# Layer 0's modulation in linear stages, seven-product down projections in the first block, rotations ahead of the heads' sums, memory in four transfers

## The chip, the cores and the metric

One core of one Trainium2 chip runs the kernel: TensorE (PE) multiplies, VectorE (DVE), ScalarE (ACT) and GpSimd (POOL) do the elementwise work, SyncE (SP) issues the transfers from HBM. The metric is the device time of one execution in microseconds. The kernel before takes 2530.83 us, the median of 3 runs (2528.49 to 2532.82).

## The reference

Batch 1, T=256 tokens, D=1024, all in fp32. A first block of two layers works on `x` with a memory `mem` of 256 tokens: a mixer (layer 0 forgetting and differential attention, layer 1 an mLSTM), attention over the memory, and a convolutional FFN; then a final norm. A second block of two layers works on `x` and a context `ctx` (512 tokens together), with three branches (latent attention MLA, grouped attention GQA, a Fourier branch), gates, and again an FFN; each of its norms and residual additions is modulated by vectors computed from the conditions `c` and `c_ctx`.

```python
for layer in range(2):                    # first block
    x = x + mixer[layer](rms_norm(x, mix_norm[layer]))
    x = x + memory_cross_attention(rms_norm(x, xattn_norm[layer]),
                                   rms_norm(mem, mem_norm[layer]), wq, wkv, wo)
    x = x + conv_ffn(rms_norm(x, ffn_norm[layer]), w_up, conv_w, conv_b, w_down)
def conv_ffn(xn, w_up, conv_w, conv_b, w_down):
    h = causal_depthwise_conv(xn @ w_up, conv_w) + conv_b
    g, u = jnp.split(h, 2, axis=-1)
    return (jax.nn.gelu(g) * u) @ w_down  # d_ff = 2816
# second block, each layer: mod = silu(c) @ w_mod + b_mod, cut into shift, scale
# and gate vectors of D for the mixer and the FFN, for x by c, for ctx by c_ctx
```

## The kernel before, in words

**Order of work.** Each engine has a list of parts in program order (`prog`, filled by `add(tensor=..., vector=...)`); semaphores order them between engines. Activations lie as [128 features, 8 tiles, tokens] in `X`. Weights come in slabs of at most 32 tiles of 128x128 (2048 KB; a down slab has 44) in two slots. SP issues all transfers in program order: `load(g)` waits (`slot_free`) until slab g-2 is used up, and everything written behind a wait of SP waits too. Slabs: 0 to 3 memkv0 (keys and values of the memory), 4 to 9 foxin (mixer input), 10 memv0, 11 and 12 mixout0, 13 memk0, 14 and 15 xq0, 16 and 17 xo0, 18 memk1, then up and down of FFN a0; later layer 1 with a1, and the second block with b0 and b1.

**Linear stages.** `tensor_linear` (L548, its matmuls L569) goes through jobs of two output tiles, 16 matmuls of 128x256 each, in four PSUM banks; `reads_linear` reads a job's bank on VectorE or ScalarE (L1504, L1507, L1642). An fp32 matmul is two records of the profile. A norm squares on ScalarE (L446), sums on POOL (L480, L487) and TensorE (L436), takes the root with a refinement on VectorE (L518 to L529) and scales there (L508); `add_norm_within` (L1578) puts a norm inside the job of another matrix (memk0, memk1), so that TensorE has work beside it.

**Start.** SP issues the memory (1024 KB) first, then the small columns, the first slab in halves, x, slab 1. Five matmuls on ones (L2944) warm TensorE up; VectorE waits for the last and then multiplies the memory by its gains (`vector_mem_gain`, L1956), eight instructions, which the first job of memkv0 follows. Later `tensor_start`, `scalar_start` and `vector_start` (L1905 to L1932) compute the differential attention's lambda with exponentials.

**Modulation of layer 0.** It has 48 tiles; for each, a 512 KB piece of w_mod (`load_mod`) and two products with a sum (128x1024) on VectorE, one for c, one for c_ctx (`vector_mod_product`, L619). All of it lies in the FFN stages a0 and a1, 24 tiles each: four turns in the up loop (`vector_mod_turn`), more in its last part (`vector_mod_tile`) and the rest between the reads of the down stage (`add_out`). c (1024 KB) comes at the beginning of each up stage, and ScalarE takes its silu (L819). Four slots hold pieces.

**FFN.** The up projection is done with seven products instead of eight (`tensor_up_seven`, L750 and L769; sums on VectorE and POOL). The down projection of b0 and b1 too: for each of four pairs of output tiles, seven products of 11 tiles of 128x128 with 128 columns (`tensor_down_seven`, L1029), whose sums of weights are made by POOL (`gpsimd_down_sums`) and VectorE (`vector_down_seven`). The down projection of a0 and a1 is plain: 8 output tiles by 22 matmuls of 256 columns (`add_out`, L569), with the norm that follows a1 (the context's) behind its first job.

**Heads (second block).** After the low-rank projections come rotations ("R", L2354), the sums of squares of the heads with root and refinement, V's products ("V", L1529), spreads of the roots to the rows ("S", L2548), each followed by a scaling on VectorE (`vector_out`, L2558), and units of the Fourier branch ("four", L2578, L2589). The order is written out by hand:

```python
early = [("R", "QG", 0), ("R", "QG", 1), ("four",), ("R", "QG", 2), ("R", "QG", 3)]
middle = [("R", "QR", 0), ("R", "QR", 1), ("V",), ("four",), ("four",)]
order = [("S", "KG", 0), ("S", "KR", 0), ("four",), ("S", "KR", 1), ("turn",), ("four",),
         ("R", "KG", 0), ("S", "KN", 0), ("four",), ("S", "KN", 1), ("S", "KN", 2), ("four",), ("S", "KN", 3)]
```

`early` runs before the sums of squares, `middle` beside root and refinement, `order` after it. Layer 0 treats 512 tokens and has eight Fourier units, layer 1 has four. V is the value product of the latent attention, 16 records of 512 columns; its second half needs a bank that holds a QR rotation's product until VectorE has multiplied that by the sines (L2365), which stands behind root and refinement in VectorE's order.

Of the kernel before, what the change touches and what calls it, by code (L numbers as in the profile page):

```python
# [19 lines left out]
ALU = mybir.AluOpType  # L20
# [4 lines left out]
D = 1024  # L25
DK = D // P
T = 256
# [226 lines left out]
def two_blocks(nc, x_in, mem_in, ctx_in, c_in, small_in, weights_in, mod_in, out, known):  # L254
# [6 lines left out]
    with ExitStack() as ctx:  # L261
# [4 lines left out]
        for n in ("tensor_done", "scalar_done", "vector_done", "gpsimd_done",  # L266
                  "landed0", "landed1", "mod_landed0", "mod_landed1", "mod_landed2", "mod_landed3", "late_landed0", "late_landed1", "loaded_c", "landed_first", "landed_second", "loaded_x", "loaded_mem", "loaded_ctx", "loaded_small", "loaded_rest",
                  "conv_done", "mod_done", "stored"):
            sems[n] = ctx.enter_context(nc.semaphore(n))
# [3 lines left out]
        CD, MD = "conv_done", "mod_done"  # L273
# [46 lines left out]
        MODC = H[:, 0:DK, T:2 * T].rearrange("p (g j) t -> p g j t", g=2)  # L320
        MODP = H[:, DK:DK + 4, T:2 * T]
        mod_slots = [area(15360 + D * i, 4, T) for i in range(4)]
# [285 lines left out]
        MOD_LOOP, MOD_HALF = 4, MOD_TILES // 2  # L608

        def mod_slot(r):  # L610
            return 0 if r < MOD_LOOP else (r - MOD_LOOP + 1) % 4

        def mod_landed(f, r):

            before = [mod_slot(i) for _ in range(f) for i in range(MOD_HALF)] + [mod_slot(i) for i in range(r + 1)]
            return sems[f"mod_landed{mod_slot(r)}"], 16 * before.count(mod_slot(r))
# [4 lines left out]
        def vector_mod_turn(dve, s, g, turn):  # L621

            f = int(s[1])
            if g == 0:
                sem, landed = mod_landed(f, 0)
                dve.wait_ge(sem, landed + 16 * turn)
                dve.wait_ge(*of(s, "mod_kept", turn=turn, back=1))
            w = mod_slots[0]
            vector_mod_product(dve, w, MODC[:, g, :, :], tiny[:, 48 + g:49 + g], w if g else MODP)\
                .then_inc(*tick(MD, s, "mod_product", g))  # L630
            if g:
                dve.wait_ge(*of(s, "mod_product", 1, turn=turn))
                dve.tensor_copy(MOD[:, 0, bass.ds(turn + MOD_HALF * f, 1), :],
                                tiny[:, 48:50].rearrange("p (m g) -> p m g", g=2)).then_inc(*tick(MD, s, "mod_kept"))

        def vector_mod_tile(dve, s, r, g):
            f = int(s[1])
            w = mod_slots[mod_slot(r)]
            if g == 0:
                dve.wait_ge(*mod_landed(f, r))  # L640
                if r > MOD_LOOP:
                    dve.wait_ge(*of(s, "mod_tile", r - 1, 0))
            vector_mod_product(dve, w, MODC[:, g, :, :], MOD[:, 0, MOD_HALF * f + r, g:g + 1], w if g else MODP)\
                .then_inc(*tick(VD, s, "mod_tile", r, g))
# [169 lines left out]
        def scalar_up_seven(act, s, segs):  # L814
            n, _, centre = conv_spec(s[0], segs)
            h = n // 2
            if s[0] == "a":
                act.wait_ge(sems["loaded_c"], 16 * (int(s[1]) + 1))
                act.activation(MODC, MODC, ACT.Silu).then_inc(*tick(SD, s, "silu_c"))  # L819

# [29 lines left out]
        def vector_up_seven(dve, s, norm, segs):  # L850
# [49 lines left out]
            def body(i, turn, m):  # L900
# [26 lines left out]
                if s[0] == "a" and turn is not None:  # L927
                    if i == 0:
                        dve.wait_ge(*of(s, "silu_c"))
                    if i % 2 == 0:  # L930
                        vector_mod_turn(dve, s, i // 2, turn)
                elif s[0] == "a" and i >= W_LAST and i % 2 == 0:
                    vector_mod_tile(dve, s, MOD_LOOP, (i - W_LAST) // 2)
# [2348 lines left out]
```

## Time and profile before

| | us |
|---|---|
| median of 3 runs | 2530.83 |
| lowest, highest | 2528.49, 2532.82 |
| profiled execution | 2534.89 |
| its span | 2533.0 |
| TensorE busy | 2481.1 (98%) |
| VectorE busy | 1272.5 (50%) |
| ScalarE, POOL busy | 542.8, 551.2 |

The profile is of one execution. Its span counts from its first to its last instruction; the 1.9 us around it belong to the time alone. Times in the timeline count from the span's start. A row names the engine, the line, the operation, what it writes and reads, and in brackets how long the engine had been idle and whose signal ended that.

### The profile page before, as it was taken

Reading aid. Unit: us, or ns where it says so; the run is one execution under the profiler, and the core shown is the slowest. Engines: PE = TensorE matmul, PEld = TensorE weight load, DVE = VectorE, ACT = ScalarE, POOL = GpSimd, SP = SyncE. Lnnn points to the kernel's source line nnn. Section 1 sums busy time; section 2 is a strip of 40 time slices with the busy share of each in tenths; the row PEclk is TensorE's granted clock in tenths of the full one; section 3 lists DMA queues with packets and bytes.
Section 4 is the critical chain, followed back from the end, with each engine's and each line's share of the span. In section 5 each row is a group of like instructions: output and inputs, shape, how many; then the busy total and the mean of one; then the engine's idle time right before and its main releaser. Section 6 shows DMA issues by size and latency. Waiting matters only on the chain.

```text
span 2533.0 us, 36719 instructions
## 1 busy us (share of the span) xinstructions
PE 2481.1 (98%) x14004; PEld 2023.3 (80%) x14004; DVE 1272.5 (50%) x2606; ACT 542.8 (21%) x1193; POOL 551.2 (22%) x474
## 2 busy tenths in 40 slices
PE   9989999999999999999999999999999999999999
PEld 6857889986799998644567766888888875899999
DVE  4034168851325887323846763554551246435774
ACT  1131122112212220213630001222200215212220
POOL 1000135200212540001002321322241010232543
PEclk9999999999999999999999999999999999999999
DMA  6323264653334566120014562121222120244443
GB/s 234 133 100 116 83 223 177 250 197 133 115 135 167 191 224 232 67 92 27 1 77 146 218 245 113 67 99 66 112 92 80 67 94 26 101 158 158 166 191 109
DMA packets 39970, 334.59 MB, mean 132 GB/s; under 512 B 3872, under 2 KB 10144, under 8 KB 22688
## 3 DMA queue, kind: packets, MB, share of 16 engines
q1 hardware_dynamic: 39840, 332.78, 35.5%
q8 instruction: 91, 1.49, 0.2%
q14 instruction: 39, 0.32, 0.0%
HBM read 331.72 MB, written 1.05 MB: 131 GB/s over the span
## 4 chain that ended last, share of the span: by engine, by line
PE 92%; DVE 4%; DMA 2%; POOL 1%; issue 1%; ACT 1%; DVEq 0%; SPq 0%; POOLq 0%; ACTq 0%
PE PS L769 24%; PE PS L569 21%; PE PS L2756 7%; PE PS L1029 6%; PE PS L1529 5%; PE PS L1719 4%; PE PS L2797 4%; PE PS L1338 3%; PE PS L1704 3%; PE PS L2276 2%; PE PS L1349 2%; PE PS L1361 2%; PE PS L436 1%; DMA slot<-in_weights 1%; PE PS L750 1%; PE PS L2414 1%
## 5 line engine op out<-in xcount | busy, mean ns | idle before, releaser
L769 PE MATMUL PS<-SQ,slot 128*128 128x128 f32 (+1 forms) x1984 | 294.5, 301 | 3.7 <-DVE slot L865 3.7
L569 PE MATMUL PS<-XN,slot 128*128 128x256 f32 (+1 forms) x1184 | 296.8, 411 | 0.8 <-DVE XN L508 0.8
L769 PEld LDWEIGHTS PS<-SQ,slot 128*128 128x128 f32 x1984 | 268.1, 191 | 17.1 <-DVE slot L865 4.2
L569 PEld LDWEIGHTS PS<-XN,slot 128*128 128x128 f32 x1184 | 224.4, 190 | 69.9 <-issue 42.5
L769 PE MATMUL PS<-XN,slot 128*128 128x128 f32 (+1 forms) x1664 | 250.0, 301 | 0.0
L569 PE MATMUL PS<-arena,slot 128*128 128x256 f32 x1088 | 237.0, 379 | 1.6 <-DVE arena L1956 1.5
L769 PEld LDWEIGHTS PS<-XN,slot 128*128 128x128 f32 x1664 | 226.1, 192 | 10.7
L569 PEld LDWEIGHTS PS<-arena,slot 128*128 128x128 f32 x1088 | 206.2, 190 | 31.8 <-DVE arena L1956 2.3
L892 DVE SCALAR_TENSOR_TENSOR arena<-PS,small,arena 128x255 f32<-128x255 f32 (+2 forms) x352 | 174.8, 543 | 45.8 <-ACT arena L836 44.6
L836 ACT ACTIVATE arena<-PS,small 128x256 f32<-128x256 f32 (+1 forms) x176 | 105.3, 616 | 380.1 <-DVE PS L925 244.0
L480 POOL TENSOR_TENSOR SQ<-SQ 128x512 f32<-128x512 f32 (+1 forms) x36 | 42.4, 1184 | 540.5 <-ACT SQ L446 539.9
L1029 PE MATMUL PS<-arena,slot 128*128 128x128 f32 (+1 forms) x846 | 130.6, 314 | 1.3 <-DVE arena L1103 0.8
L1029 PEld LDWEIGHTS PS<-arena,slot 128*128 128x128 f32 x846 | 119.9, 191 | 10.0 <-DVE arena L1103 1.0
L446 ACT ACTIVATE SQ<-X 128x512 f32<-128x512 f32 (+1 forms) x68 | 36.1, 551 | 410.3 <-DVE X L1642 172.2
L619 DVE CUSTOM_DVE_ANT_1 arena<-arena 128x1024 f32<-128x1024 f32 x96 | 121.2, 1310 | 4.5 <-DMA arena<-in_mod 4.3
L2756 PE MATMUL PS<-arena,slot 128*128 128x256 f32 (+1 forms) x704 | 119.6, 328 | 1.7 <-DVE slot L2880 1.5
L2756 PEld LDWEIGHTS PS<-arena,slot 128*128 128x128 f32 x704 | 107.0, 191 | 12.1 <-DVE slot L2880 3.0
L769 PE MATMUL PS<-SQ,probs 128*128 128x128 f32 (+1 forms) x704 | 111.4, 301 | 1.3 <-DVE SQ L877 1.3
L1719 PE MATMUL PS<-arena,slot 128*128 128x128 f32 (+1 forms) x688 | 110.1, 321 | 0.0
L950 POOL TENSOR_TENSOR slot<-slot 128x512 f32<-128x512 f32 x84 | 109.4, 1302 | 0.0
L1719 PEld LDWEIGHTS PS<-arena,slot 128*128 128x128 f32 x688 | 101.4, 191 | 8.4 <-issue 0.5
L962 POOL TENSOR_TENSOR arena<-arena 128x256 f32 (+3 forms) x88 | 79.9, 908 | 113.0 <-ACT arena L845 113.0
(289 smaller groups left out, 3669.6 us busy)
## 6 DMA issues: line engine op xcount, KB each, us to landing
slot<-in_weights SPq DMA_DIRECT2D x85, 2048.0 KB, 7.8
arena<-in_mod SPq DMA_DIRECT2D x96, 512.0 KB, 3.6
slot<-in_weights SPq DMA_DIRECT2D x16, 2816.0 KB, 9.8
slot<-in_weights SPq DMA_DIRECT2D x24, 1536.0 KB, 6.8
slot<-in_weights SPq DMA_DIRECT2D x5, 1024.0 KB, 4.8
slot<-in_weights SPq DMA_DIRECT2D x2, 2176.0 KB, 8.8
arena<-in_c SPq DMA_DIRECT2D x3, 1024.0 KB, 10.4
small<-in_small SPq DMA_DIRECT2D x1, 1982.0 KB, 17.7
```

The lines of the kernel that those rows point to most:

```text
L569: mm = pe.matmul(o, l, r, start=k == 0, stop=k == len(terms) - 1, skip_group_check=True)
L619: return dve.tensor_tensor_reduce(scratch, w, c, 1.0, 0.0, ALU.mult, ALU.add, total)
L769: mm = pe.matmul(PS[:, bank, 0:h], lhs[:, k * P:(k + 1) * P], rhs(k), start=first and k == 0, stop=last and k == 3, skip_group_check=True)
L836: act.activation(hb[:, half, :], src[half], ACT.Identity, bias=conv_col(s, m - 1, half, 3), scale=conv_col(s, m - 1, half, centre))\
L892: op = dve.scalar_tensor_tensor(out=o[:, :, lo:hi], in0=x[:, :, lo + d:hi + d], scalar=conv_col(s, m - 1, half, c), in1=o[:, :, lo:hi], op ...
L950: pool.tensor_tensor(a21, a11, a21, ALU.subtract).then_inc(*w_tick(s, GD, "s3", i, turn))
L962: pool.tensor_tensor(dst, hb[:, 0, :], hb[:, 1, :], ALU.mult).then_inc(*w_tick(s, GD, "h", i, turn))
L1029: mm = pe.matmul(d_psum(p, what, h), lhs[:, k * P:(k + 1) * P], rhs(k), start=k == 0, stop=k == KH - 1, skip_group_check=True)
L1529: mm = pe.matmul(PS[:, bank, 0:cols_n], lhs(k, t), r, start=k == 0, stop=k == k_tiles - 1)
L1719: mm = pe.matmul(PS[:, bank_of(m), part[g]], w[:, a:a + P], rhs(k, part[g]), start=k == 0, stop=k == k_tiles - 1, skip_group_check=True)
L2756: mm = pe.matmul(PS[:, bank, 0:hq], lhs[:, k * P:(k + 1) * P], rhs[:, k, 0:hq], start=first and k == 0, stop=last and k == 3, skip_group_c ...
L2797: mm = pe.matmul(PS[:, BBR + i, 0:nq], slot[:, a:a + P], BR[b][:, k, 0:nq], start=k == 0, stop=k == 3, skip_group_check=True)
```

## The change

1. The modulation of layer 0 leaves the stages of a0 and a1. `vector_mod_tiles` does tiles 0 to 6 behind `vector_start`; 7 to 11, 12 and 13 to 17 before the reads of foxin's jobs 2, 3 and 6; 18 to 23 behind job 7; 24 to 29 in twos before the reads 0 to 2 of mixout0; 30 to 39 behind the memk0 read; 40 to 47 in twos before the reads of xo0. There are two slots, so that `load_mod(n)` waits for tile n-2. SP issues them behind the slabs as `MOD_LOADS` says. c comes twice, behind slab 2 and, once the mixer's last sub-norm output is there, behind slab 12.
2. The down projections of a0 and a1 go by seven products as b's do, with `tensor_tensor` where b has a gate; POOL makes pair 0's first sum at the end of the up stage. The context norm in a1 is behind pair 0.
3. In the heads the two rotations of QR stand before the sums of squares, V right behind them; the Fourier units are spread anew (so many of them as there are parts of the tokens) and one comes behind the last spread.
4. At the start the small columns go first, the memory in four transfers of 256 KB, each with its own semaphore, three of them behind the first half slab; three warm-up matmuls instead of five; the gains are shared by VectorE and ScalarE, and VectorE waits for the warm-up after its own. ScalarE begins with a square of one column.

```diff
+        MODC = [X[:, :, T:2 * T].rearrange("p (g j) t -> p g j t", g=2), area(12288, 2, 4, T)]
+        mod_slots = [area(16384 + D * i, 4, T) for i in range(2)]
+        MOD_LOADS = {g: [] for g in range(len(table))}
+        for g, n in zip((3, 4, 5, 6, 7, 8, 9, 10, 12, 13, 14, 15, 16, 17, 18), (4, 3, 3, 3, 3, 3, 3, 2, 4, 4, 2, 3, 4, 6, 1)):
+            done = sum(len(v) for v in MOD_LOADS.values())
+            MOD_LOADS[g] = list(range(done, done + n))
+        def vector_mod_tiles(dve, *tiles):
+            for n in tiles:
+                w = mod_slots[n % 2]
+                c = MODC[n // MOD_HALF]
+                if n % MOD_HALF == 0:
+                    dve.wait_ge(*of("silu_c", n // MOD_HALF))
+                dve.wait_ge(sems[f"mod_landed{n % 2}"], 16 * (n // 2 + 1))
+                for g in range(2):
+                    if g == 0 and n:
+                        dve.wait_ge(*of("mod_tile", n - 1, 0))
+                    vector_mod_product(dve, w, c[:, g, :, :], MOD[:, 0, n, g:g + 1], w if g else MODP)\
+                        .then_inc(*tick(VD, "mod_tile", n, g))
+        def scalar_silu_c(act, f):
+            act.wait_ge(sems["loaded_c"], 16 * (f + 1))
+            act.activation(MODC[f], MODC[f], ACT.Silu).then_inc(*tick(SD, "silu_c", f))
...
-        def tensor_down_seven(pe, s, pairs, n):
+        def tensor_down_seven(pe, s, pairs, n, then=None):
...
+                if then and p == 0:
+                    then(pe)
...
+                if gate is None:
+                    return dve.tensor_tensor(x, src, x, ALU.add)
...
-            if p == 0 and s == "b1":
+            if p == 0 and s != "b0":
                 return
...
+            add(tensor=lambda pe: tensor_down_seven(pe, s, DK // 2, n, tensor_then),
+                vector=lambda d: vector_down_seven(d, s, DK // 2, n, gate, vector_then),
+                gpsimd=lambda p: gpsimd_down_seven(p, s, DK // 2, n))
...
                 def vector_mem_gain(dve):
-                    dve.wait_ge(sems["loaded_mem"], 16)
-                    for m in range(DK):
+                    for m in range(0, DK, 2):
+                        dve.wait_ge(sems[f"loaded_mem{m // 2}"], 16)
                         dve.tensor_scalar(MEMG[:, m, :], MEM[:, m, :], col("mem_norm0", m), None, ALU.mult)\
                             .then_inc(*tick(VD, "memnorm", "gain", m))
+                    dve.wait_ge(*of("warmed", WARM - 1))
+                def scalar_mem_gain(act):
+                    for m in range(1, DK, 2):
+                        act.wait_ge(sems[f"loaded_mem{m // 2}"], 16)
+                        act.activation(MEMG[:, m, :], MEM[:, m, :], ACT.Copy, scale=col("mem_norm0", m))\
+                            .then_inc(*tick(SD, "memnorm", "gain", m))
...
                 add(scalar=scalar_start, vector=vector_start, tensor=tensor_start)
+                add(scalar=lambda a: scalar_silu_c(a, 0), vector=lambda d: vector_mod_tiles(d, *range(0, 7)))
...
+                        vector_mod_tiles(dve, *{2: range(7, 12), 3: (12,), 6: range(13, 18)}.get(j, ()))
+                        reads_linear(dve, VD, "vector", "foxin", [job], j)
+                    vector_mod_tiles(dve, *range(18, MOD_HALF))
...
+                        [(24, 25), (26, 27), (28, 29), ()])
...
+                add(vector=lambda d: vector_mod_tiles(d, *range(30, 40)))
                 add_linear("xq0", q_jobs)
...
+                        [(40, 41), (42, 43), (44, 45), (46, 47)])
...
+            early = [("R", "QG", 0), ("R", "QG", 1), ("four",), ("R", "QG", 2), ("R", "QG", 3), ("R", "QR", 0), ("R", "QR", 1)]
+            middle = [("V",)] + [("four",)] * (len(segs) - 1)
+            order = [("S", "KG", 0), ("S", "KR", 0)] + [("four",)] * ((len(segs) - 1)) + [("S", "KR", 1), ("turn",), ("four",)]
+            order += [("R", "KG", 0), ("S", "KN", 0)] + [("four",)] * ((len(segs) - 1)) + [("S", "KN", 1), ("S", "KN", 2)]
+            order += [("four",)] * ((len(segs) - 1)) + [("S", "KN", 3), ("four",)]
...
+        WARM = 3
...
+            def load_mod(n):
+                if n >= 2:
+                    sp.wait_ge(*of("mod_tile", n - 2, 1))
+                sp.dma_start(mod_slots[n % 2], mod_in[n].rearrange("p (j t) -> p j t", t=T))\
+                    .then_inc(sems[f"mod_landed{n % 2}"], 16)
...
                     load(g, len(table[g][1]), piece(g))
+                if g == 2:
+                    load_c(0)
+                if g == first_slab["mixout0"] + 1:
+                    sp.wait_ge(*of("subln", "out", 3, 0))
+                    load_c(1)
+                for n in MOD_LOADS[g]:
+                    load_mod(n)
```

## Rows read from the trace of the kernel before

**Rows 1.** The page: span, and the chain that ended last by engine

```profile
span 2533.0 us, 36719 instructions
...
PE 92%; DVE 4%; DMA 2%; POOL 1%; issue 1%; ACT 1%; DVEq 0%; SPq 0%; POOLq 0%; ACTq 0%
```

**Rows 2.** Timeline of the start: start us, us, engine, line, operation, [idle before <-releaser]

```profile
1.45 7.56 PE L2944 MATMUL PS<-rms 128*128 128x512 f32 x10 [1.45 <-DVE rms L2955]
...
9.04 4.76 DVE L1956 TENSOR_SCALAR arena<-SQ,small 128x256 f32<-128x256 f32 x8 [7.65 <-PE PS L2944]
...
12.27 6.25 PE L569 MATMUL PS<-arena,slot 128*128 128x256 f32 x26 [0.41 <-DVE arena L1956]
```

**Rows 3.** Transfers: queue, number, KB each, median us from issue to landing

```profile
slot<-in_weights SPq DMA_DIRECT2D x85, 2048.0 KB, 7.8
...
arena<-in_mod SPq DMA_DIRECT2D x96, 512.0 KB, 3.6
...
SQ<-in_mem SPq DMA_DIRECT2D x1, 1024.0 KB, 5.9
```

**Rows 4.** Timeline around foxin's start, and the silu of c later

```profile
69.94 1.28 ACT L1932 ACT_TABLE_LOAD   x1
...
71.44 0.16 DVE L1916 TENSOR_TENSOR tiny<-tiny 128x1 f32<-128x1 f32 x1 [28.73 <-ACT tiny L1932]
...
72.89 37.39 PE L569 MATMUL PS<-XN,slot 128*128 128x256 f32 x172
...
339.31 1.91 ACT L819 ACTIVATE arena<-arena 128x2048 f32<-128x2048 f32 x1 [12.02 <-DMA arena<-in_c]
```

**Rows 5.** Timeline of the first down stage: modulation products, a slab and mod loads

```profile
514.60 0.33 SPq L2972 DMA_DIRECT2D slot<-in_weights  x1
...
514.98 15.69 SPq L2978 DMA_DIRECT2D arena<-in_mod  x6
...
516.36 2.27 DVE L619 CUSTOM_DVE_ANT_1 arena<-arena 128x1024 f32<-128x1024 f32 x1
...
525.64 1.23 DVE L619 CUSTOM_DVE_ANT_1 arena<-arena 128x1024 f32<-128x1024 f32 x1 [2.41 <-DMA arena<-in_mod]
...
526.79 1.22 DVE L619 CUSTOM_DVE_ANT_1 arena<-arena 128x1024 f32<-128x1024 f32 x1
```

**Rows 6.** Timeline: mixout0 and memk0, xq0, cross attention's first reduce

```profile
210.56 27.79 PE L569 MATMUL PS<-arena,slot 128*128 128x256 f32 x128
...
247.35 27.86 PE L569 MATMUL PS<-XN,slot 128*128 128x256 f32 x128 [0.79 <-DVE XN L508]
...
277.93 0.69 DVE L1269 TENSOR_REDUCE pair_min<-PS 128x2 f32<-128x512 f32 x1 [27.31 <-PE PS L1169]
```

**Rows 7.** Heads of both layers (timeline), and the clock of one stretch (windows)

```profile
1171.05 5.40 PE L1529 MATMUL PS<-slot,arena 128*128 128x512 f32 x8 [2.31 <-DVE arena L2365]
...
1194.01 4.30 PE L1338 MATMUL PS<-arena 64*128 64x512 f32 x16 [1.05 <-DVE arena L2558]
...
2090.59 3.70 PE L1529 MATMUL PS<-slot,arena 128*128 128x512 f32 x8 [2.37 <-DVE arena L2365]
...
core 0: us, PE busy (x) PEld busy (x) DVE busy (x) ACT busy (x) POOL busy (x), PEclk, DMA share, GB/s
1172.00:1173.00 1.00, 1.00 (x2) 0.36 (x2) 0.00 (x0) 0.00 (x0) 0.00 (x0) 0.50 0.00 0
```

**Rows 8.** The first block's down stage (chain) and b1's (timeline)

```profile
476.58 79.43 PE PS L569 x368
...
2458.62 5.08 PE L1029 MATMUL PS<-arena,slot 128*128 128x128 f32 x44
...
2519.58 9.99 PE L1029 MATMUL PS<-arena,slot 128*128 128x128 f32 x88
```

**Rows 9.** Timeline: the up stages' first summed products, a0 and b1

```profile
341.95 1.06 PE L769 MATMUL PS<-XN,slot 128*128 128x128 f32 x8
...
2325.99 1.06 PE L769 MATMUL PS<-XN,slot 128*128 128x128 f32 x8
```

More of the change, by code:

```diff
@@ L605, in conv_spec @@
             return n, taps, centre
[L608 to L616, printed above, removed]
+        MOD_HALF = MOD_TILES // 2
+        MOD_LOADS = {g: [] for g in range(len(table))}
@@ L1128, in vector_down_seven @@
                 add_to_x(p, 0, 1, ps["p3"]).then_inc(*tick(VD, d, "read", 2 * p, 1))
+                if then and p == 0:
+                    then(dve)
         def gpsimd_down_sums(pool, s, p):
@@ L1627, in add_ffn @@
                 return
-            if block == "b":
-                add(tensor=lambda pe: tensor_down_seven(pe, s, DK // 2, n),
-                    vector=lambda d: vector_down_seven(d, s, DK // 2, n, gate),
-                    gpsimd=lambda p: gpsimd_down_seven(p, s, DK // 2, n))
-                return
-            add_out(f"d{s}", lambda k: H[:, k, 0:T * len(segs)], None, FM, segs, gate,
-                    then=(lambda pe: tensor_norm(pe, aside_s, aside_units)) if aside else None,
-                    needs=lambda k: (s, "h", k) if k >= FM - 2 else (s, "h", PAIRS - 1, "last"),
-                mod=s if block == "a" else None)
@@ new lines, in add_ffn, with add_out @@
+            add(tensor=lambda pe: tensor_down_seven(pe, s, DK // 2, n, tensor_then),
+                vector=lambda d: vector_down_seven(d, s, DK // 2, n, gate, vector_then),
+                gpsimd=lambda p: gpsimd_down_seven(p, s, DK // 2, n))
+        def add_out(s, rhs, ready, k_tiles, segs, mod):
+            def reads(j, bank):
+                return [("vector", lambda e: e.tensor_tensor(
+                    X[:, 2 * j:2 * j + 2, 0:T], PS[:, bank, :].rearrange("p (i t) -> p i t", i=2),
+                    X[:, 2 * j:2 * j + 2, 0:T], ALU.add))]
+            jobs = feature_jobs(rhs, ready, DK, reads, k_tiles=k_tiles, segs=segs)
@@ L2213, in two_blocks @@
             if l == 0:
-                add_out("xo0", lambda k: O1[:, k, :], lambda k: ("xatt0", "out", k // 2), DK, [0])
+                add_out("xo0", lambda k: O1[:, k, :], lambda k: ("xatt0", "out", k // 2), DK, [0],
+                        [(40, 41), (42, 43), (44, 45), (46, 47)])
                 units = norm_x(s, X, XN, lambda m, g: col("ffn_norm0", m), after_out("xo0", [0], None), [0])
@@ L2226, in two_blocks @@
                 if l == 1 else None)
-            prev_ready = after_out(f"da{l}", [0], None)
+            prev_ready = [[(f"da{l}", "read", 2 * p, 1)] for p in range(DK // 2)]
         add_norm("final", norm_x("final", X, X, lambda m, g: col("final_norm", m), prev_ready, [0]))
@@ L2942, in _ @@
             pe.wait_ge(*of("warm"))
-            for _ in range(5):
+            for _ in range(WARM):
                 pe.matmul(PS[:, 7, :], RT[:, 0, 0:P], RT[:, 0, :], start=True, stop=True).then_inc(*tick(TD, "warmed", _))
@@ L3047, in _ @@
                         sp.dma_start(slots[0][:, half], piece(0)[:, half]).then_inc(sems[sem], 16)
+                        for m in range(1, DK // 2) if i == 0 else ():
+                            load_mem(m)
                     sp.dma_start(slots[0][:, 2 * DK * P:4 * DK * P], piece(0)[:, 2 * DK * P:4 * DK * P])\
```

142 lines of the change are left out of this document (32 added, 110 removed).

## The prediction

> **What bounds the kernel now.** I read the page first: TensorE is busy for 98% of a span of 2533.0 us and holds 92% of the chain that ended last [rows 1]. So an edit pays only where it takes matmuls, a wait of TensorE or a stretch of low clock away, and whatever makes TensorE wait costs in full. Then I read the timeline at each place that the diff touches and asked which wait ends last there. The profiled execution took 2534.89 us, 4.06 above the median of 2530.83; terms are worked out in its frame and put on the median at the end.
>
> **Start.** Five warm-up products (10 records) run from 1.45 to 9.01, and VectorE's eight gains wait for them, 9.04 to 13.80 [rows 2]. The first job's remaining 26 records end at 18.52 [rows 2]. Afterwards three products remain: 6 records at 0.85 us (in 7.56 us there is room for some seven at that spacing, at the low clock, and three at half of it) end near 6.6. The memory's 1 MB took 5.9 us [rows 3]; four quarters with the first half slab between them should be there by 8.5, and the gains, now shared by two engines, follow each quarter. The first job is 32 records at 0.217 (37.39 for 172 [rows 4]): 6.9 us, from 6.6 it could end at 13.5; the last squares and their sums come some half a microsecond later, so I take 14.1. Gain 4.4; ends 2.5 (quarters land late) and 5.
>
> **Linear stages, where the 48 tiles go.** A tile is two products, whose starts lie 1.15 apart (525.64 and 526.79) [rows 5]: 2.3 us; 48 of them are 110 us of a VectorE that is half idle. What counts is what SyncE does: it issues everything in program order, and `load_mod(n)` waits for tile n-2. Every slab behind such a wait is held.
> (a) The first slab of foxin. Tiles 0 and 1 come behind the lambda exponentials, which end at 71.4 [rows 4]. The silu needs a table load (1.28, as every table load of the profile) and 1.91 [rows 4]: 74.6. Tile 0 ends at 76.95, tile 1 at 79.25, and only then are mod loads 2 and 3 out and slab 4 issued, at 79.65 (in the kernel before it went as soon as its slot was free, at 55). A slab takes 7.8 [rows 3], and half a transfer of 512 KB is ahead of it: 88.3. TensorE wants it at 72.89 [rows 4]. **+15.4**. Nothing covers it: every later product of foxin is behind the same slab. The next slabs are issued some 12 us apart, each of 13.8 us of matmuls, and are in time.
> (b) Mixout0 [rows 6]. c (1 MB) lies behind slab 12, lands some 10 us after 210.8; with the silu the first tile starts at 223.4, two tiles go before each of three reads, and read 3 comes some 2.8 us after its 238.4; the memory keys' first half hides part. **+1.6** (0 to 3).
> (c) Second slab of xq0. Its load waits for tile 31, two tiles behind the memk0 read, whose end I call R. Issued at R+5.0, behind a mod load, lands at R+13.7. TensorE wants it after two jobs of xq0, 247.35+13.9, which with R=250.6 is R+10.7 [rows 6]. **+3.0**.
> (d) Cross attention. Ten tiles, 30 to 39, stand on VectorE ahead of its first reduce. Alone they take 23 us, but a mod transfer goes in order with the slabs: one issued at 514.98, just behind a slab issued at 514.60, was used only at 525.64, 10.7 us later against 3.6 from issue to landing [rows 3, 5]. Following tile by tile through two slabs, tile 39 ends at R+36; the reduce was wanted at 277.93 [rows 6], R+27.3, now R+30.3 with (c). **+5.8**.
> Fox pairs: VectorE ends tile 23 some 2.9 us before its first score is there, so no cost, but no cover beyond that. xo0 has two tiles (4.6) and a read (0.69) in 6.9 us a job: hidden. In all 25.8.
> POOL's share: a product that met a sum of POOL took 2.27 where others take 1.21 to 1.23 [rows 5], so +1.06 for one meeting. The norm at mixout0 brings three; I take 0 in the sum, since two of the three fall in VectorE's waits, and 3.2 for the upper end. The Trainium skill, page "SBUF — State Buffer", section "🔬 SBUF: two separate sides", says that the port pair which VectorE and GpSimd share is locked by one instruction for its whole length and that the loser fully blocks. By it all three meetings cost a whole POOL sum each, and the forecast would stand some 3 us higher, at 2540; the trace agrees in kind, with its 1.06.
> (e) Clock after the new waits. In heads 0 TensorE waited 2.31 us and then needed 5.40 for what takes 3.70 in layer 1; the granted clock in that stretch is 0.50, the level of 1.2 GHz [rows 7]. So 1.7 for a wait. (a), (c) and (d) make three: **+5.1**; ends 0 (layer 1's wait of 2.37 shows no dip) and 8.
>
> **Up stages.** a0's runs from 341.95 to 476.58, 134.6; b1's, which has no modulation beside it, from 2325.99 to 2458.62, 132.6 [rows 8, 9]. So a0 gains 1.8 (2.0, less 0.2 because the two starts are marked at the end of different norms). a1 keeps the context's load: 0.6, between 0 and 1.8.
>
> **Down projections.** A plain one is 8x22 products of 256 columns, 352 records at 0.216 (79.43 for 368): 76.0 us [rows 8]. Seven products for each of four pairs, 11 tiles of 128 columns: 616 records at 0.1122 (88 in 9.99 [rows 8], whose last one's drain is counted once), 69.1. b1's, of the same size, took 2458.62 to 2529.57, 70.95, with one short stall in the first pair [rows 8]. a0: **-5.05**. Its sums on VectorE and POOL replace the mod tiles that stood there, and b1 shows that they fit. In a1 the context norm goes behind pair 0: some 7 us of VectorE and 3 of POOL in front of pair 1's sums; pair 1 has 17 us. I take 0.75 lost: **-4.3**, ends 0 and -5.
>
> **Heads.** The rotations of QR go ahead of the sums of squares, and V's second half no longer waits for VectorE: 2.31 and 2.37 [rows 7]. The dip of 1.7 in layer 0 goes with it. The wait of 1.05 for the last normalized tile at 1194.01 [rows 7] is covered by one Fourier unit put behind its spread; layer 1 has about the same. Late next: the reciprocal root, ready 0.9 later; TensorE has all of V, twice the 3.5 of these rows, before it needs it (in layer 0 a Fourier unit too), and reaches the first spread about 1.8 later than the root. Layer 0 -5.0, layer 1 -3.6: **-8.6**, ends -4 and -9.
>
> **Sum**: +25.8 +5.1 -4.4 -1.8 -0.6 -5.05 -4.3 -8.6 = +6.2: 2541.1 in the profiled frame, 2537.0 on the median.
>
> **Rivals.** 0.2%, 5.1 us, is about what a measurement of this kernel can tell from no change: faster is under 2525.8, slower over 2535.9.
> 1, the other side: mod transfers don't wait for slabs. Then c and mods land 3.6 us or so after issue, the ten tiles end at R+24 to R+27 and (b) and (d) are gone, with (d)'s dip; the shorter waits then leave the clock alone: -1.6 -5.8 -1.7 -3.4 = 2524.5. It decides at tile 39: before R+30.3 TensorE doesn't wait. For it: 16 engines, DMA busy for a small share here; against: the row at 525.64. 0.2.
> 2: seven products in a0 and a1 gain nothing, because VectorE and POOL, still on the up stage's tail, feed pair 0 late and the context norm delays pair 1: +9.4, 2546.4. Against: b1. 0.08.
> 3: VectorE late at the fox pairs. Tiles of 2.6 instead of 2.3 (transfers behind slabs, POOL) are +7.2 over 24 tiles, less 2.9: +4.3, 2541.3. 0.12.
> 4: the heads gain half, because the first spread then waits for the root: +4.3, 2541.3. For it: only 1.8 us of slack in layer 0. 0.1.
> 5: the change doesn't do what it says at foxin: if tiles 0 and 1 ran in VectorE's idle 28.73 us [rows 4], slab 4 would go out at 55 and (a) be gone with its dip: 2519.9. Against: they stand behind the exponentials in VectorE's order. 0.05.
> Forecast 0.45, with a range of its own from 2532 to 2541. Slower: 0.28 of the forecast and 0.08, 0.1, 0.08 of rivals 2 to 4, 0.54; faster: 0.13 of rival 1 and 0.05 of rival 5, 0.18; the rest, 0.28, within. Range 2523 to 2546: from rival 1 with a little more to rival 2.
>
> **What would show it.** TensorE idle about 15 us before foxin (released by the slab), 3 in xq0's middle and 6 at the first reduce of cross attention; granted clock 0.5 behind them; down stages of 71 and 72 us; V's products in the heads without a wait before them; the norm's matmuls near 14. Wrong if slab 4 is issued before 64, or the down stages stay at 76.

## The result, and the profile after

The changed kernel takes 2540.51 us, the median of 7 runs (2536.48 to 2542.60), against 2532.22 for the kernel before beside it (7 runs, 2528.49 to 2533.30). The ratio is 1.0034 with a 95% interval of 1.0023 to 1.0046: slower by 8.6 us (5.8 to 11.6). The forecast was 6.2 slower. The profiled execution took 2538.87, 4.0 more than the profiled one of before; the two medians are 8.3 apart, because one execution of before lay 2.7 above its median and one of after 1.6 below. So the profiles show where the terms are; their sum to within some 4 us.

The page of the changed kernel, lines that answer to [rows 1]:

```profile
span 2537.1 us, 37955 instructions
...
PE 87%; DVE 5%; DMA 4%; issue 2%; ACT 1%; POOL 1%; SPq 0%; POOLq 0%; DVEq 0%
```

TensorE's share of the chain has fallen from 92% to 87%, transfers and VectorE have taken it. Where the time went, the same instructions of the two timelines show (start of the first instruction named, us):

| stage begins with | before | after | shift | step | forecast |
|---|---|---|---|---|---|
| memory keys behind the first norm | 19.65 | 16.52 | -3.1 | start -3.1 | -4.4 |
| foxin | 72.89 | 84.60 | +11.7 | (a) +14.8 | +15.4 |
| value products of foxin | 128.25 | 142.72 | +14.5 | clock +2.8 | +1.7 |
| mixout0 | 210.56 | 225.08 | +14.5 | 0 | 0 |
| norm behind mixout0 | 241.64 | 259.90 | +18.3 | (b) +3.7 | +1.6 |
| first reduce of cross attention | 277.93 | 305.16 | +27.2 | (c) +3.1 with clock, (d) +5.8 | +4.7, +7.5 |
| xo0 | 292.54 | 320.32 | +27.8 | +0.6 | 0 |
| up a0, first summed products | 341.95 | 368.18 | +26.2 | -1.6 | 0 |
| down a0 | 476.42 | 501.07 | +24.6 | -1.6 | -1.8 |
| memk2, behind down a0 | 552.39 | 571.80 | +19.4 | -5.2 | -5.05 |
| down a1 | 936.51 | 955.30 | +18.8 | -0.6 | -0.6 |
| second block | 1016.36 | 1032.17 | +15.8 | -3.0 | -4.3 |
| attention behind heads 0 | 1194.01 | 1204.64 | +10.6 | -5.2 | -5.0 |
| attention behind heads 1 | 2105.26 | 2110.58 | +5.3 | -1.7 in between, -3.6 | -3.6 |
| end of the span | 2533.0 | 2537.1 | +4.1 | -1.2 in b1 | 0 |

The timeline of the changed kernel at foxin (start us, us, engine, line, operation, what ended the idle time), against [rows 4]:

```profile
69.59 1.91 ACT L637 ACTIVATE X<-X 128x2048 f32<-128x2048 f32 x1
71.53 1.23 DVE L618 CUSTOM_DVE_ANT_1 arena<-arena,X 128x1024 f32<-128x1024 f32 x1 [2.87 <-ACT X L637]
...
73.94 2.62 SPq L2963 DMA_DIRECT2D arena<-in_mod  x2
76.61 0.43 SPq L2955 DMA_DIRECT2D slot<-in_weights  x1
...
84.60 40.58 PE L569 MATMUL PS<-XN,slot 128*128 128x256 f32 x174 [14.78 <-DMA slot<-in_weights]
```

Silu, two tiles, two pieces, then the slab, and TensorE 14.78 us behind it: the chain of the forecast, some 3 us earlier by the start's gain. The clock behind that wait, by windows:

```profile
core 0: us, PE busy (x) PEld busy (x) DVE busy (x) ACT busy (x) POOL busy (x), PEclk, DMA share, GB/s
84.00:94.00 10.00, 9.40 (x31) 7.84 (x32) 7.27 (x13) 0.00 (x0) 0.00 (x0) 0.69 0.76 294
```

A granted clock of 0.69 over ten microseconds: a part of them was at 1.2 GHz. Mixout0, the same timeline:

```profile
225.65 0.43 SPq L2958 DMA_DIRECT2D arena<-in_c  x1
...
236.91 1.91 ACT L637 ACTIVATE arena<-arena 128x2048 f32<-128x2048 f32 x1 [9.73 <-DMA arena<-in_c]
238.85 1.22 DVE L618 CUSTOM_DVE_ANT_0 arena<-arena 128x1024 f32<-128x1024 f32 x1 [13.91 <-ACT arena L637]
...
250.62 2.34 POOL L480 TENSOR_TENSOR SQ<-SQ 128x512 f32<-128x512 f32 x1 [225.12 <-ACT SQ L446]
...
251.77 2.28 DVE L618 CUSTOM_DVE_ANT_0 arena<-arena 128x1024 f32<-128x1024 f32 x1
...
257.69 1.26 POOL L480 TENSOR_TENSOR SQ<-SQ 128x512 f32<-128x512 f32 x1 [4.73 <-ACT SQ L446]
...
259.90 1.91 PE L436 MATMUL PS<-SQ,small 128*128 128x256 f32 x6 [3.58 <-POOL SQ L487]
```

c takes 11.3 us behind slab 12, the tiles are 0.9 later than forecast, two of them wait for their pieces (0.48, 0.74), and one meets POOL's sum and takes 1.06 more. Behind the wait of 3.58 that ends at 259.90, the matmuls from 260.8 to 264.2 run at half their rate. Then xq0 and cross attention:

```profile
274.31 0.43 SPq L2955 DMA_DIRECT2D slot<-in_weights  x1
...
282.56 14.05 PE L569 MATMUL PS<-XN,slot 128*128 128x256 f32 x64 [2.17 <-DMA slot<-in_weights]
...
297.03 1.23 DVE L618 CUSTOM_DVE_ANT_0 arena<-arena 128x1024 f32<-128x1024 f32 x1 [5.35 <-DMA arena<-in_mod]
...
305.16 1.28 DVE L1257 TENSOR_REDUCE pair_min<-PS 128x2 f32<-128x512 f32 x2
306.95 3.78 PE L1157 MATMUL PS<-arena 128*128 128x256 f32 x8 [4.21 <-ACT probs L1210]
...
307.00:312.00 5.00, 5.00 (x15) 4.15 (x16) 1.99 (x6) 2.25 (x11) 4.00 (x5) 0.50 0.69 288
```

Slab 15 is issued between two pieces and is 2.17 late; the tiles wait for pieces behind slabs (5.35 for one), and the first reduce comes at 305.16, 5.8 later than the shift of its scores. The last line is of the windows view (its columns as above): behind the wait of 4.21 TensorE is granted 0.50, 1.2 GHz, for five microseconds. Of the gains, the start and the heads ([rows 2, 7] before):

```profile
7.45 7.64 PE L569 MATMUL PS<-arena,slot 128*128 128x256 f32 x32 [1.45 <-DMA slot<-in_weights]
...
15.12 1.56 PE L436 MATMUL PS<-SQ,small 128*128 128x256 f32 x6
...
1180.85 7.13 PE L1517 MATMUL PS<-slot,arena 128*128 128x512 f32 x16
...
2093.39 7.13 PE L1517 MATMUL PS<-slot,arena 128*128 128x512 f32 x16
```

The value products of both heads run in one piece, with no wait and no dip. At the start the first job now waits for the first half slab, to 7.45, where the forecast had it begin at 6.6. In a1's down stage, pair 0:

```profile
959.78 2.65 POOL L480 TENSOR_TENSOR SQ<-SQ 128x512 f32<-128x512 f32 x1
...
961.22 2.68 DVE L1070 TENSOR_TENSOR arena<-arena 128x1408 f32<-128x1408 f32 x1
...
963.83 2.69 DVE L1075 TENSOR_TENSOR slot<-arena,slot 128x1408 f32<-128x1408 f32 x1
964.00 2.69 PE L1011 MATMUL PS<-arena,slot 128*128 128x128 f32 x22 [1.17 <-DVE arena L1070]
...
968.68 2.69 PE L1011 MATMUL PS<-arena,slot 128*128 128x128 f32 x22 [1.98 <-DVE arena L1078]
```

VectorE's sums of 1408 elements take 1.61 in a0 and 2.68 here, where POOL adds squares for the context's norm at the same time; TensorE waits 1.17, 1.98 and 0.72, in a0 0.38 and 0.73.

### The profile page after: what moved, and what is told of

It reads as the page before. It is cut to its first block, busy times and chain, and to the rows that moved or that the text cites. A ratio compares the mean times of both kernels' runs of the same rounds, so it can differ in the third digit from the quotient of the medians.

```text
span 2537.1 us, 37955 instructions
## 1 busy us (share of the span) xinstructions
PE 2468.0 (97%) x14528; PEld 2031.6 (80%) x14528; DVE 1340.0 (53%) x2707; ACT 547.6 (22%) x1200; POOL 597.9 (24%) x488
## 4 chain that ended last, share of the span: by engine, by line
PE 87%; DVE 5%; DMA 4%; issue 2%; ACT 1%; POOL 1%; SPq 0%; POOLq 0%; DVEq 0%
PE PS L762 25%; PE PS L569 12%; PE PS L1011 11%; PE PS L2732 6%; PE PS L1517 5%; PE PS L1677 4%; PE PS L2773 4%; PE PS L1326 3%; PE PS L1662 3%; PE PS L2251 2%; DMA slot<-in_weights 2%; DMA arena<-in_mod 2%; PE PS L1337 2%; PE PS L1349 2%; PE PS L436 1%
## 5 line engine op out<-in xcount | busy, mean ns | idle before, releaser
L762 PEld LDWEIGHTS PS<-SQ,slot 128*128 128x128 f32 x1984 | 268.3, 192 | 14.1 <-DVE slot L854 1.5
L1011 PE MATMUL PS<-arena,slot 128*128 128x128 f32 (+1 forms) x1902 | 251.5, 293 | 6.3 <-DVE arena L1078 2.7
L1011 PEld LDWEIGHTS PS<-arena,slot 128*128 128x128 f32 x1902 | 239.2, 192 | 16.0 <-DVE arena L1078 3.2
L762 PEld LDWEIGHTS PS<-XN,slot 128*128 128x128 f32 x1664 | 226.4, 192 | 10.6
L618 DVE CUSTOM_DVE_ANT_0 arena<-arena 128x1024 f32<-128x1024 f32 x112 | 146.7, 1352 | 57.4 <-DMA arena<-in_mod 43.5
L2732 PEld LDWEIGHTS PS<-arena,slot 128*128 128x128 f32 x704 | 107.2, 191 | 12.1 <-DVE slot L2856 3.0
L1677 PE MATMUL PS<-arena,slot 128*128 128x128 f32 (+1 forms) x688 | 110.1, 321 | 0.0
L932 POOL TENSOR_TENSOR slot<-slot 128x512 f32<-128x512 f32 x84 | 108.2, 1288 | 0.0
L1677 PEld LDWEIGHTS PS<-arena,slot 128*128 128x128 f32 x688 | 101.5, 191 | 8.3 <-issue 0.5
L2877 POOL TENSOR_TENSOR slot<-slot 128x512 f32<-128x512 f32 x22 | 29.9, 1357 | 330.3 <-DMA slot<-in_weights 330.3
L762 PEld LDWEIGHTS PS<-SQ,probs 128*128 128x128 f32 x704 | 97.8, 192 | 5.9 <-DVE SQ L866 1.4
```

What stands on the lines that cost most here:

```text
L618: return dve.tensor_tensor_reduce(scratch, w, c, 1.0, 0.0, ALU.mult, ALU.add, total)
L762: mm = pe.matmul(PS[:, bank, 0:h], lhs[:, k * P:(k + 1) * P], rhs(k), start=first and k == 0, stop=last and k == 3, skip_group_check=True)
L932: pool.tensor_tensor(a21, a11, a21, ALU.subtract).then_inc(*w_tick(s, GD, "s3", i, turn))
L1011: mm = pe.matmul(d_psum(p, what, h), lhs[:, k * P:(k + 1) * P], rhs(k), start=k == 0, stop=k == KH - 1, skip_group_check=True)
L1677: mm = pe.matmul(PS[:, bank_of(m), part[g]], w[:, a:a + P], rhs(k, part[g]), start=k == 0, stop=k == k_tiles - 1, skip_group_check=True)
L2732: mm = pe.matmul(PS[:, bank, 0:hq], lhs[:, k * P:(k + 1) * P], rhs[:, k, 0:hq], start=first and k == 0, stop=last and k == 3, skip_group_c ...
```

## The experiments

Ratios are to the kernel before, beside which each ran; 0.001 is 2.5 us. The kernel before had medians from 2529.57 to 2532.22 in the different rounds, so that a difference of medians across rounds can be 2 to 3 us off the difference of ratios; both are given where they part. The first four runs: two parts alone, one undone, and the largest wait taken away.

**slab4_free.** Its edit:

```diff
-        ... (4, 3, 3, 3, 3, 3, 3, 2, 4, 4, 2, 3, 4, 6, 1)):
+        ... (2, 5, 3, 3, 3, 3, 3, 2, 4, 4, 2, 3, 4, 6, 1)):
```

> The changed kernel with two modulation pieces behind slab 3 instead of four and five behind slab 4 instead of three, so that SyncE waits for no tile before it issues slab 4. Theory (the order of the transfers holds the slab): slab 4 is issued near 51 and there when TensorE wants it near 69.8; the wait of 14.8 us and the clock dip of 2.8 behind it are gone, 17.6 us less than the changed kernel, about 9 us below the kernel before. If tiles 2 to 6 then come later, the first reads of foxin may give 1 to 3 back. Rival (the transfers themselves, not their order, are short of bandwidth here): slab 4 lands late all the same and at most 5 us are won.

Measured: 2535.20 us, 1.0013 (1.0003 to 1.0022), 5.3 less than the changed kernel, where I had expected 17.6. Slab 4 is in time (foxin starts at 69.54), so the rival falls too. The timeline has both the reason and the wait:

```profile
69.54 14.08 PE L569 MATMUL PS<-XN,slot 128*128 128x256 f32 x64
...
73.72 11.76 SPq L2963 DMA_DIRECT2D arena<-in_mod  x5
...
85.53 0.43 SPq L2955 DMA_DIRECT2D slot<-in_weights  x1
...
93.56 16.67 PE L569 MATMUL PS<-XN,slot 128*128 128x256 f32 x63 [9.94 <-DMA slot<-in_weights]
```

Now five pieces stand between slabs 4 and 5, slab 5 waits for tile 4, and TensorE waits 9.94 at the next slab, with the same 2.8 of low clock behind it (16.67 for 63 records that take 13.8). With VectorE starting its tiles at 71, moving pieces from before slab 4 to behind it only moved the wait to slab 5.

**heads_alone.** Its edit, on the kernel before:

```diff
-            middle = [("R", "QR", 0), ("R", "QR", 1), ("V",), ("four",), ("four",)]
+            early += [("R", "QR", 0), ("R", "QR", 1)]
+            middle = [("V",)] + [("four",)] * (len(segs) - 1)
...
```

> The kernel before with the new order of rotations, value products and Fourier units in the heads and nothing else. Theory of the prediction: 8.6 us less. The trace of the changed kernel shows more in layer 0 (the shift between the two kernels goes from +15.8 to +8.9 over layer 0's heads and attention, 6.9, and by 3.6 in layer 1), so 10.5 less if that is the order's doing. Rival: part of the 6.9 is the clock of one execution, and the edit alone gives 5 to 7.

Measured: 2521.35 us, 0.9962 (0.9948 to 0.9976), 9.6 less. The same row as in the changed kernel:

```profile
1159.19 7.13 PE L1529 MATMUL PS<-slot,arena 128*128 128x512 f32 x16
```

The interval, 6.1 to 13.2 less, holds 8.6, 10.5 and the upper end of the rival, so the time alone decides nothing. The trace does: from the second block's start to the attention layer 0 takes 172.45 here, 177.65 before and 172.47 in the changed kernel, 5.2 less, and layer 1's heads are 3.6 shorter, 8.8 together. The further 1.7 of my expectation lies between the attention of layer 0 and layer 1, with which the edit has nothing to do. There this kernel takes 1.4 more than the one before, where the changed kernel took 1.7 less: that is the difference between executions, as the rival said.

**down_plain.** a0's and a1's down projections as before:

```diff
+            if block == "a":
+                add_out(f"d{s}", lambda k: H[:, k, 0:T], lambda k: None, FM, segs, [(), (), (), ()], tensor_then, needs)
+                return
             add(tensor=lambda pe: tensor_down_seven(pe, s, DK // 2, n, tensor_then),
```

> The changed kernel with a0's and a1's down projections plain again (352 records of 256 columns each), all else as changed. Theory: a0 longer by 5.1, a1 by 2.6 to 4.3 (by the trace of the changed kernel its stage lasts 74.7 against 77.3), so 7.7 to 9.4 us slower than the changed kernel. Rival: the sums on VectorE and POOL delay what comes next by as much as the matmuls save; then the two are equal within 2 us.

Measured: 2549.18 us, 1.0070 (1.0054 to 1.0086), 9.1 more than the changed kernel by the ratios and 8.7 by the medians. The sum stands, at the upper side of the expectation.

**start_alone.** The new start on the kernel before (the whole fourth part of the change, nothing else).

> The kernel before with the new start alone (small columns first, memory in four transfers, gains on two engines, three warm-up products, the table loaded early). Prediction: 4.4 us less, ends 2.5 and 5. By the trace of the changed kernel 3.1 less: the first job waits for the first half slab until 7.45, not for the warm-up. Rival: the clock is lower later because of fewer warm-up products, and less than 1.5 us is left.

Measured: 2530.31 us, 0.9995 (0.9985 to 1.0005), 1.3 less, between 3.8 less and 1.3 more. The forecast's 4.4 is outside the interval, and 1.3 is the size that the rival named. In its trace the value products of foxin start 3.2 earlier than in the kernel before (125.07 against 128.25). But the old start is not the same in every execution: heads_alone has it unchanged, and there

```profile
1.45 6.09 PE L2945 MATMUL PS<-rms 128*128 128x512 f32 x10 [1.45 <-DVE rms L2956]
...
17.32 2.97 PE L569 MATMUL PS<-arena,slot 128*128 128x256 f32 x13
```

the ten warm-up records take 6.09 instead of 7.56 [rows 2], and the memory keys begin at 17.32 instead of 19.65. They begin at 16.47 here, 0.85 earlier than in heads_alone and 3.2 earlier than in the kernel before; over all traces at 19.65, 19.62 and 17.32 with the old start and at 16.3 to 17.9 with the new. So the gain is 0.9 to 3.2 by the execution that it is compared with. That goes with the small difference of the medians without any later loss of clock, which was the rival's reason and isn't shown.

**tiles_spread.** On the changed kernel:

```diff
-        ... zip((3, 4, 5, 6, 7, 8, 9, 10, 12, 13, 14, 15, 16, 17, 18), (4, 3, 3, 3, 3, 3, 3, 2, 4, 4, 2, 3, 4, 6, 1)):
+        ... zip((2, 3, 4, 5, 6, 7, 8, 9, 12, 13, 14, 15, 17), (3, 2, 4, 4, 2, 4, 2, 8, 4, 1, 1, 6, 7)):
...
-                c = MODC[n // MOD_HALF]
+                c = MODC[n >= 33]
...
+                add(scalar=lambda a: scalar_silu_c(a, 0), vector=lambda d: vector_mod_tiles(d, *range(0, 12)))
                 add_tokens("memkv0", ...)
...
```

> The changed kernel with its 48 tiles elsewhere and nothing else: c and three pieces already behind slab 2, twelve tiles in VectorE's idle stretch before the lambda exponentials (39.6 to 68.3), one behind them, fourteen in foxin, six in mixout0 (with the first copy of c, so that they don't wait for the second), seven before cross attention, eight in xo0; the number of pieces behind each slab is chosen so that no slab is issued later than 8 us before it is wanted. Theory (all four waits come from SyncE's order, and a wait taken away does not come back because no other slab is held in its place): the waits of 14.8, 3.6, 2.2 and 5.8 us and the clock dips of 2.8 and 0.7 behind them are gone, 29 us less than the changed kernel, about 2512, 0.992 of the kernel before. Rival (24 MB more in the first 350 us are too much for the transfers, and the wait moves on as it did from slab 4 to slab 5): at most 10 us less than the changed kernel.

Measured: 2530.34 us, 0.9993 (0.9985 to 1.0002), 10.2 less than the changed kernel instead of 29. That is the size of the rival too, but not for its reason. The trace of it:

```profile
53.85 0.33 SPq L2956 DMA_DIRECT2D slot<-in_weights  x1
...
85.26 0.56 PE L1881 MATMUL PS<-tiny,small 128*128 128x2 f32 x2 [17.71 <-DVE tiny L1869]
85.75 5.78 PE L569 MATMUL PS<-XN,small 128*8 128x256 f32 x16
```

No slab is late (slab 4 goes out at 53.85), and from foxin to the FFN TensorE has no wait for a transfer over 1.5 us. But the lambda sums need one small product that VectorE makes behind the twelve early tiles, and TensorE waits 17.71 us for it: my own edit had made a new wait.

**ctx_norm_later.** On the changed kernel:

```diff
-                if then and p == 0:
+                if then and p == 1:
                     then(pe)
...
             for p in range(1, pairs):
                 gpsimd_down_sums(pool, s, p)
+                if at == p:
+                    then(pool)
```

> The changed kernel with the context's norm in a1's down stage one pair later: its sums on POOL behind pair 1's, its matmuls and VectorE's part behind pair 1 too. In the changed kernel VectorE's sums of pair 0 stand beside POOL's sums of that norm: two of them take 2.7 us instead of 1.6, and TensorE waits 1.17, 1.98 and 0.72 where a0 waits 0.38 and 0.73. Theory (the two engines get in each other's way there): a1's stage is 2.8 us shorter if the same does not happen in pair 2, so 1 to 3 us less than the changed kernel. Rival: the norm's place does not matter, 0.

Measured: 2535.99 us, 1.0019 (1.0009 to 1.0029), 3.8 less than the changed kernel by the ratios, 4.5 by the medians. Its down a1 lasts from 950.72 to 1022.74, 72.0 against 74.7, and the waits are a0's again:

```profile
961.42 2.69 PE L1011 MATMUL PS<-arena,slot 128*128 128x128 f32 x22 [0.38 <-DVE arena L1078]
...
964.84 10.09 PE L1011 MATMUL PS<-arena,slot 128*128 128x128 f32 x88 [0.72 <-DVE arena L1089]
...
971.01 2.68 POOL L480 TENSOR_TENSOR SQ<-SQ 128x512 f32<-128x512 f32 x2
...
972.51 2.65 DVE L1075 TENSOR_TENSOR slot<-arena,slot 128x1408 f32<-128x1408 f32 x1 [2.16 <-PE PS L1011]
```

POOL and VectorE still meet in pair 1 (2.65 again), but the sum that is slow there is not waited for.

**linear_alone.** The changed kernel with the second, third and fourth part taken back: the modulation in the linear stages and nothing else.

> The kernel before with the first part of the change alone: modulation in the linear stages, none in the FFN stages; down projections plain, old heads, old start. Theory by the traces: waits and dips in the linear stages +29 to +31, up stages -1.8, -0.6 and -1.5 at a0's start, so +26 to +28 us, 1.0105. By adding the single parts up (changed kernel +8.6, heads -9.6, down about -8.6, start -1.3): +28. Rival (the parts are not additive, the waits overlap with what the other parts do): below +20.

Measured: 2559.10 us, 1.0112 (1.0096 to 1.0129), 28.3 more. The parts add up: 28.3 - 9.6 - 9.1 - 1.3 = 8.3, and the whole is 8.6. That they meet so closely is luck, since the intervals reach 2.5 to 4 us to either side of each; what is shown is that no large overlap is hidden.

**spread_later.** The two last edits together.

> Tiles spread and the context's norm a pair later, together, on the changed kernel. Theory: the sum of the two, 30 to 32 us less than the changed kernel, near 2510. Rival: no better than the spread tiles alone.

Measured: 2526.63 us, 0.9983 (0.9975 to 0.9992): 3.7 less by the medians, 2.5 by the ratios, than with spread tiles alone, so the norm's place pays again; the 17.7 of the lambda sums are in it too.

**spread_products_first.** On tiles_spread, one instruction moved:

```diff
-                add(scalar=lambda a: scalar_silu_c(a, 0), vector=lambda d: vector_mod_tiles(d, *range(0, 12)))
+                add(scalar=lambda a: scalar_silu_c(a, 0), vector=lambda d: (vector_start(d), vector_mod_tiles(d, *range(0, 12))))
...
-                add(scalar=scalar_start, vector=vector_start, tensor=tensor_start)
+                add(scalar=scalar_start, vector=vector_lambda, tensor=tensor_start)
```

where `vector_start` keeps the products (and a memset of one column) and `vector_lambda` has what follows the exponentials.

> The kernel with spread tiles, with one instruction moved: VectorE makes the lambda products ahead of the twelve early tiles instead of behind them. In the trace of the spread kernel no slab is late any more, but TensorE waits 17.7 us at the lambda sums for that one product, which I had left behind the tiles in VectorE's order, and the 16 gate matmuls behind that wait take 5.8 us instead of 3.6. Theory (the expected 29 us were all given back at that one place): 18 to 20 us less than the spread kernel, 2510 to 2513, 28 to 30 less than the changed kernel. Rival (the early tiles really cost the time, since VectorE ends them only at 85 and the fox gates and reads behind them are late): at most 10 us less than the spread kernel.

Measured: 2509.85 us, 0.9922 (0.9908 to 0.9935): by the medians 20.5 less than the spread kernel and 30.7 less than the changed one, by the ratios 18.0 and 28.3.

```profile
66.30 0.28 PE L1883 MATMUL PS<-tiny,small 128*128 128x2 f32 x2
66.50 3.62 PE L569 MATMUL PS<-XN,small 128*8 128x256 f32 x16
...
70.05 40.20 PE L569 MATMUL PS<-XN,slot 128*128 128x256 f32 x185
```

No wait at the sums, the gate matmuls at 3.62 again, and foxin at full clock. VectorE still ends its early tiles only at 87, and nothing waits for that. From the start of the memory keys to xo0 this kernel takes 272.90 us (16.81 to 289.71), the kernel before 272.89 (19.65 to 292.54) and the changed kernel 303.80 (16.52 to 320.32): the modulation in these stages costs TensorE nothing any more.

**spread_products_later.** The same with the context's norm a pair later.

> The same with the context's norm one pair later too. Theory: another 2.7 to 4.5 us less, as on the changed kernel and on the spread one, so 2506 to 2510, about 0.991 of the kernel before. Rival: equal to the run beside it.

Measured: 2505.14 us (2504.52 to 2506.68), 0.9902 (0.9886 to 0.9917): 24.8 us below the kernel before by the ratio (24.4 by the medians), 33 to 35 below the changed one, and the best of all. Against the run beside it 4.7 less by the medians, 5.1 by the ratios. Its page:

```profile
span 2502.7 us, 37954 instructions
...
PE 91%; DVE 4%; DMA 2%; issue 1%; POOL 1%; ACT 1%; SPq 0%; POOLq 0%; DVEq 0%
```

## Why the prediction was right, and where its steps were off

**The linear stages** decided it, as forecast. The steps (a) to (e) came to 30.9 in the forecast and to 30.9 in the trace (from -3.1 at the start to +27.8 at xo0), but not term by term; that the two sums are equal is luck, for (b) was forecast 2.1 too low and (a), (c) and (e) together some 2 too high. (a) was 14.8 against 15.4. (b) was 3.7 against 1.6: I had laid c's landing a microsecond too early and had counted no meeting with POOL; there was one, of 1.06, on the path. (c) was 2.3, against 3.0, with 0.8 of clock ahead of it. (d) was 5.8, as worked out tile by tile.

(e), the clock, was 2.8 behind (a), 0.8 ahead of (c), and at most 0.6 behind (d), some 4 in all against 5.1. The step had a dip of 1.7 behind each of the waits (a), (c) and (d), and each costing in full. The trace has dips of other sizes and in other places, and hides most of them. Behind the wait of 3.58 in mixout0's norm, which the step didn't count, the matmuls lost 1.7, of which 0.8 reached the path, because in the kernel before xq0 waits 0.79 at that place anyway. Behind (c)'s 2.17 they lost nothing (granted clock 1.00 from 282 to 286). Behind TensorE's 4.21 in cross attention 16 records at twice their spacing lost 2.5, of which at most 0.6 was left at xo0. Nor is a dip behind a given wait a fixed price: the waits of 2.31 and 2.37 in the heads' old order, from which the step took its 1.7, have it in layer 0 alone in the kernel before, in layer 1 alone in linear_alone and in both layers in start_alone.

That none of it is a lack of bandwidth was argued there and is shown by spread_products_first: the same 48 pieces and tiles, transferred and multiplied in another order in which no slab stands behind a late tile, and the whole 30.9 of the stages is gone. What caused each wait is shown less evenly. For (a) and (c) a slab's place behind a tile is the cause in the rows. For (b) and (d) the same edit also changed how many tiles stand ahead of a read (seven instead of ten before the first reduce) and which copy of c they need, and the runs don't part that from SyncE's order.

One sentence of step (a) had a hole. "The next slabs are issued some 12 us apart, each of 13.8 us of matmuls, and are in time" was right only because slab 4 was already late; slab4_free has slab 4 in time, and then slab 5 isn't. The held slab was not the cause but the first place where the cause, tiles that start at 71, showed.

**Up and down stages.** Down a0 (-5.2) came as forecast, up a1 (-0.6) too, and both repeat to 0.1 in every trace that has them. Up a0's -1.6 looks as good against -1.8, but is luck: that stage takes 134.5 in the kernel before and 131.5 and 132.0 in heads_alone and start_alone, which have it unchanged, and 131.3 to 134.0 in the kernels without modulation there. What the tiles cost in it is below what single executions tell. Down a1 was the mis-sized term: -2.6 in the stage itself against -4.3. The step had priced the norm's VectorE and POOL work as delay behind pair 0; the loss was inside pair 0, where POOL's three sums lie beside VectorE's sums of weights. ctx_norm_later moved them and got 2.7 back in that stage. Its time fell by 3.8, and by 2.5 to 5.1 in the two pairs of runs on the spread tiles; whether there is more to it than the stage shows, these runs leave open.

**Where VectorE and POOL met.** Each of VectorE's weight sums that met one of POOL's sums of 512 elements took 1.07 more; the tile beside POOL at mixout0 took 1.06 more. POOL's sums of 512 elements, alone 1.26, took 2.34, 2.65 and 2.16 in these meetings. So POOL lost not a fixed amount but what was left of VectorE's instruction: at mixout0 the product that began with POOL's sum kept its 1.23 and ended at 251.84, POOL's sum ended 1.12 behind it, at 252.96, and the product that VectorE had begun at 251.77 ended 1.08 behind that. The Trainium skill, page "SBUF — State Buffer", section "🔬 SBUF: two separate sides", says that the shared port pair is held by one of the two for a whole instruction while the other fully blocks. The trace agrees: 1.06 and 1.07 are all but 0.2 of POOL's sum of 1.26. What the forecast had wrong was the number of meetings on the path. It had counted none; there was one at mixout0, and in a1's pair 0 there were three, of 1.07, 1.07 and 0.53 (with POOL's last, shorter sum), 2.67 together, which is what ctx_norm_later got back in the stage.

**Heads and start.** The heads gave 5.2 and 3.6 against 5.0 and 3.6. In layer 0 the new order takes 172.45 to 172.47 in all traces that have it; the old one takes 177.65 in the kernel before and 175.97 in linear_alone, which has no dip there. So 3.5 of the 5.2 is the order's waits in any execution, and the 1.7 of clock is there in some; layer 1 gains 3.6 or 5.3 in the same way. The start gave 3.1 against 4.4 between the two profiled executions, and as little as 0.8 against heads_alone. The step had the transfers too early: the first half slab let the first job begin at 7.45 instead of 6.6, and the last quarter of the memory came at 9.95 instead of 8.5, so that the norm's matmuls began at 15.1 instead of 14.1.

**Not forecast**: the stretch from xo0 to up a0's first summed products, 1.6 shorter. No cause is shown. In the kernel before, c and four pieces are fetched there beside the first slabs, and the clock stands at 0.57 over the 8 us before 339, in the changed kernel at 0.79 over 358 to 366; but start_alone, which fetches them there too, has this stretch 0.6 shorter than the changed kernel. And 1.7 and 1.2 us in the merge of layer 0 and in b1, which the change doesn't touch. Single executions differ by as much and more: between the attention of layer 0 and that of layer 1 the nine kernels with the new order of the heads take 905.3 to 910.2 us. That is why the +4.1 of the two profiles and the 8.6 of the runs can both be right.

**The rivals.** Rival 1 (pieces that don't wait for slabs) falls by the wait of 5.35 that ends at 297.03: its piece was issued at 288.43, 1.9 behind a slab, and was used 8.6 later, not 3.6; rival 2 by down_plain; rival 3 because VectorE reached the fox pairs in time, its first reading of them 2.86 behind the scores in both kernels; rival 4 by the heads' rows; rival 5 by the slab issued at 76.61.

## What to carry to other kernels

Where one queue issues everything in program order, a wait written into it is a wait for all that follows: put the work that it waits for where its engine is idle and early, and count for each important transfer the last event that the queue has to pass before it, in the order in which it would be wanted if the wait ahead were gone. Taking away the first late transfer shows only whether the next one is late too. A stage that an edit touches is judged by several traces: some repeat to 0.1 us, others differ by 3 between executions of the same code. And before work is put into an engine's idle stretch, look for the one small instruction at the stretch's end that another engine waits for, and leave that ahead of it.

## What the runs showed of the hardware

Of a VectorE and a POOL instruction on SBUF operands that met, the one that came second waited for nearly all of what was left of the other: VectorE's product of 1024 elements took 2.28 instead of 1.22 and its sum of 1408 elements 2.68 instead of 1.61 beside POOL's sum of 512 (alone 1.26), and POOL's sum 2.34 and 2.65. A wait of TensorE of 14.8 us (changed kernel) and one of 9.9 us (slab4_free) were both followed by 2.8 us of lost clock. In the changed kernel one of 4.21 was followed by 2.5, one of 3.58 by 1.7, and one of 2.17 by none. The same wait of 2.31 cost 1.7 in the kernel before and nothing in linear_alone, and the one of 2.37 the other way round. A piece of 512 KB issued 1.9 us behind a slab of 2048 KB was used 8.6 us after its issue, against a median of 3.4 from issue to landing in the same trace.
